# Seven half-size products in place of eight for half of K in two output tile pairs of a two-layer encoder kernel

## What is computed

```python
def _spatial_gating_mixer(h, w_in, ln_g, ln_b, w_s, b_s, w_out):
    ...
    y = u * sv * jax.nn.silu(z)      # (512, 2048)
    return y @ w_out                 # w_out: (2048, 1024)
...
    x = x + gate * y                 # y is here the mixer's result
return _rmsnorm(x, final_g)
```

## Time and profile before

| | us |
|---|---|
| median of 3 runs (803.05 to 803.89) | 803.4 |
| the profiled execution: its time | 802.44 |
| the profiled execution: its span, first to last instruction | 800.6 |
| PE busy | 792.4 |
| DVE busy | 659.4 |
| ACT busy | 455.7 |

### The profile page before, as it was taken

How to read it: one execution, slowest core, us unless ns; L and a number is a source line. 1 busy time by engine, 2 the same in 40 slices (tenths; PEclk the granted TensorE clock), 3 DMA queues, 4 the chain that set the end, 5 groups by cost and what they waited for, 6 DMA issues and landing times.

```text
span 800.6 us, 15179 instructions
## 1 busy us (share of the span) xinstructions
PE 792.4 (99%) x5562; PEld 744.7 (93%) x5562; DVE 659.4 (82%) x954; ACT 455.7 (57%) x638; POOL 82.8 (10%) x108
## 2 busy tenths in 40 slices
PE   9999999999999999999999999999999999999996
PEld 8889999999999999998889888899999999988896
DVE  5989999999999999898896788978888888883334
ACT  4675656565656656572332886656767777762220
POOL 1010000000000000102201241010000000000000
PEclk9999999999999999999999999999999999999999
DMA  9996566666666666589873784255455445454103
GB/s 348 374 204 196 145 184 183 183 183 184 182 185 179 187 177 190 174 247 364 316 246 86 251 239 86 76 142 155 135 154 157 131 131 151 138 194 173 54 1 106
DMA packets 42097, 143.92 MB, mean 180 GB/s; under 512 B 5336, under 2 KB 7638, under 8 KB 42064
## 3 DMA queue, kind: packets, MB, share of 16 engines
q1 hardware_dynamic: 31760, 111.16, 38.4%
q0 software_dynamic: 9152, 30.16, 20.4%
q10 hardware_dynamic: 1152, 2.18, 0.7%
HBM read 109.14 MB, written 4.21 MB: 142 GB/s over the span
## 4 chain that ended last, share of the span: by engine, by line
PE 95%; issue 3%; DVE 1%; ACT 1%; POOL 0%; POOLq 0%; DVEq 0%
PE pp L1363 11%; PE pp L1364 11%; PE pp L1365 11%; PE pp L1222 8%; PE pp L1224 7%; PE pp L1223 7%; PE p_aux L1363 7%; PE p_aux L1364 7%; PE p_aux L1365 7%; PE pp L1318 3%; PE pp L1495 2%; PE pp L1497 2%; PE pp L1496 2%; PE p_aux L1537 2%; PE p_aux L1610 2%
## 5 line engine op out<-in xcount | busy, mean ns | idle before, releaser
L1363 PE MATMUL pp<-h_hi,wh 128*128 128x256 f32 x280 | 79.3, 283 | 0.0
L1364 PE MATMUL pp<-h_lo,wh 128*128 128x256 f32 x280 | 79.2, 283 | 0.0
L1365 PE MATMUL pp<-h_hi,wl 128*128 128x256 f32 x280 | 79.2, 283 | 0.0
L825 ACT ACTIVATE wh<-wt 128x1024 fp32r<-128x1024 f32 x56 | 58.9, 1054 | 13.7 <-DVE wt L1900 7.6
L1919 DVE TENSOR_TENSOR wl<-wt,wh 128x1024 fp32r<-128x1024 f32 x56 | 66.5, 1219 | 0.2 <-ACT wh L825 0.2
L1363 PE MATMUL pp<-s_hi,wh 128*128 128x256 f32 x224 | 63.4, 283 | 0.0
L1364 PE MATMUL pp<-s_lo,wh 128*128 128x256 f32 x224 | 63.4, 283 | 0.0
L1365 PE MATMUL pp<-s_hi,wl 128*128 128x256 f32 x224 | 63.4, 283 | 0.0
L1365 PE MATMUL p_aux<-s_hi,wl 128*128 128x256 f32 x224 | 63.4, 283 | 0.0
L1363 PE MATMUL p_aux<-s_hi,wh 128*128 128x256 f32 x224 | 63.4, 283 | 0.0
L1364 PE MATMUL p_aux<-s_lo,wh 128*128 128x256 f32 x224 | 63.4, 283 | 0.0
(11 more groups left out here) (291 smaller groups left out, 2656.3 us busy)
## 6 DMA issues: line engine op xcount, KB each, us to landing
raw<-in_stream SPq DMA_DIRECT2D x140, 512.0 KB, 4.1
wl<-raw POOLq DMA_DIRECT2D x28, 512.0 KB, 4.5
raw_l<-in_stream SPq DMA_DIRECT2D x18, 512.0 KB, 6.5
raw_s<-in_stream SPq DMA_DIRECT2D x16, 512.0 KB, 13.8
wl_b<-raw POOLq DMA_DIRECT2D x16, 512.0 KB, 4.6
raw_m<-in_stream SPq DMA_DIRECT2D x14, 512.0 KB, 3.3
xv_lo<-y POOLq DMA_DIRECT2D x6, 512.0 KB, 6.0
x_s<-in_xt SPq DMA_DIRECT2D x4, 512.0 KB, 5.9
```

The costliest lines, as they stand in the source:

```text
L825: act.activation(wh[g % 2][:, at], wt[g % 2][:, at], ACT.Copy).then_inc(t_hi_cut, 1)
L1363: pe.matmul(out, hi, hi_of(k), start=fresh and k == 0, stop=False, skip_group_check=not fresh)
L1364: pe.matmul(out, hi, lo_of(k), start=False, stop=False, skip_group_check=not fresh)
L1365: mm = pe.matmul(out, lo, hi_of(k), start=False, stop=k == 3, skip_group_check=not fresh)
```

## The change

For pairs 1 and 2, the upper half of K (K tiles 8 to 15, slots 2 and 3 of the pair) is no longer done as 48 matmuls of 512 columns. It is seen as a 2 x 2 block product: y's upper half in four parts, positions 0-255 and 256-511 by K tiles 8-11 and 12-15 (`y_part(t, kh)`), and the weights in four parts by output tile and K half. Seven products of 12 matmuls with 256 columns (`seventh`) take the place of the eight block products. Slots 0 and 1 stay as they were.

What this needs beside it:

- Once, four sums of parts of y (`s_sum_o_at`, 128x1024 each) on DVE, their high parts on ACT (`hi_s_o`) and low parts on DVE (`s_low_o`). The sums read `y32`; the low parts of K tiles 8 to 11 go to new places, while `y_low` 6 and 7 still overwrite K tiles 12 to 15 and now stand behind three of the sums.
- For each of the two pairs, four sums of weights (`t_sums_o`, one instruction of 128x1024 and two of 128x512), two high parts and two low parts of 128x1024; three copies out of PSUM on ACT (`copy_o`); on DVE the x update in five pieces instead of two.
- The partial results go to banks of `p_aux` besides the pair's own two.

The diff, cut to its core:

```diff
+        so_hi = at_kb("so_hi", 60, [P, 4, 4, HALF], F32R)
+        so_lo = at_kb("so_lo", 76, [P, 4, 4, HALF], F32R)
+        so_f = at_kb("so_f", 76, [P, 4, 4, HALF])
+        to_hi = at_kb("to_hi", 16, [P, 2048], F32R)
+        to_lo = at_kb("to_lo", 188, [P, 2048], F32R)
+        to_f = at_kb("to_f", 188, [P, 2048])
+        y_lo_4 = at_kb("y_lo_4", 24, [P, 2, S], F32R)
+        y_lo_5 = at_kb("y_lo_5", 172, [P, 2, S], F32R)
...
+        bank_a_o, bank_c_o = {1: p_aux[:, 0, :], 2: p_aux[:, 2, :]}, {1: p_aux[:, 1, :], 2: p_aux[:, 3, :]}
...
+            if layer and kt // 2 in (4, 5):
+                return (y_lo_4, y_lo_5)[kt // 2 - 4][:, kt % 2, :]
+            return y_lo[:, kt, :]
...
-            for j in range(DPAIRS - 1):
-                for s in range(4):
-                    cut_hi_late(j + W_BOUT // 4, s, 1)
-                square_x(1, j)
-            cut_hi_late(W_BOUT // 4 + DPAIRS - 1, 0, 1)
...
+            at_w = W_BOUT // 4
+            cut_hi_late(at_w, 0, 1)
+            for n in (0, 1, 3):
+                hi_s_o(n)
+            cut_hi_late(at_w, 1, 1)
+            hi_s_o(2)
+            hi_t_o(1, 0)
+            hi_t_o(1, 1)
+            cut_hi_late(at_w, 2, 1)
+            square_x(1, 0)
+            cut_hi_late(at_w, 3, 1)
+            cut_hi_late(at_w + 1, 0, 1)
+            cut_hi_late(at_w + 1, 1, 1)
+            copy_o(1, 0)
+            cut_hi_late(at_w + 1, 2, 1)
+            copy_o(1, 1)
+            copy_o(1, 2)
+            hi_t_o(2, 0)
+            hi_t_o(2, 1)
...
-            for j in range(DPAIRS - 1):
-                if j == 1:
-                    pe.wait_ge(c_sum_b, OFF + 3 * 2 * PAIRS)
-                out_product(1, W_BOUT, j)
...
+            def seventh(out, stationary, moving, fresh):
+                hi_of, lo_of = moving
+                for k in range(4):
+                    hi, lo = stationary(k)
+                    pe.matmul(out, hi, hi_of(k), start=fresh and k == 0, stop=False, skip_group_check=not fresh)
+                    pe.matmul(out, hi, lo_of(k), start=False, stop=False, skip_group_check=not fresh)
+                    mm = pe.matmul(out, lo, hi_of(k), start=False, stop=k == 3, skip_group_check=not fresh)
+                return mm
...
+            def seven_products(j):
+                a, b, c = bank_a_o[j][:, left], pp[out_bank(1, j)], bank_c_o[j][:, left]
+                for s in range(2):
+                    out_slot(1, W_BOUT, j, s)
+                    for u in range(2):
+                        if s == 0 and j != 1:
+                            pe.wait_ge(x_updated, X_STEPS + FREE + j + u)
+                        unit(pp[out_bank(1, j) + u][:, :], weights(s, u, out_ring[1]), rows(y_hi), low_rows(1),
+                             range(4 * s, 4 * s + 4), s == 0, s == 1).then_inc(blocks, 1)
+                out_slot(1, W_BOUT, j, 2)
+                seventh(a, tile_hi_lo(2, 0), y_own(0, 0), True).then_inc(prod_o, 1)
+                pe.wait_ge(s_cut_o, 1)
+                pe.wait_ge(t_cut_o, of_o(j, 2, 1))
+                seventh(c, t_hi_lo(0), y_summed(N1), True).then_inc(prod_o, 1)
+                pe.wait_ge(s_cut_o, 2)
+                pe.wait_ge(t_cut_o, of_o(j, 2, 2))
+                pe.wait_ge(copied_o, of_o(j, 3, 1))
+                seventh(a, t_hi_lo(2), y_summed(S2), False).then_inc(prod_o, 1)
+                out_slot(1, W_BOUT, j, 3)
+                seventh(b[:, left], tile_hi_lo(3, 0), y_own(0, 1), False).then_inc(prod_o, 1)
+                pe.wait_ge(s_cut_o, 4)
+                pe.wait_ge(copied_o, of_o(j, 3, 2))
+                seventh(a, t_hi_lo(1), y_summed(S3), False).then_inc(prod_o, 1)
+                seventh(b[:, right], t_hi_lo(3), y_own(1, 1), False).then_inc(prod_o, 1)
+                pe.wait_ge(c_22_o, of_o(j, 1, 1))
+                seventh(c, tile_hi_lo(3, 1), y_summed(S4), False).then_inc(blocks, 4)
+            out_product(1, W_BOUT, 0)
+            pe.wait_ge(c_sum_b, OFF + 3 * 2 * PAIRS)
+            pe.wait_ge(sv_used, 2 + KE)
+            for j in B_SEVEN:
+                seven_products(j)
...
+                out = y_lo[:, 2 * n:2 * n + 2, :]
+                if nth >= PAIRS and n in (4, 5):
+                    out = (y_lo_4, y_lo_5)[n - 4][:, :, :]
+                dve.tensor_tensor(out, y32[:, 2 * n:2 * n + 2, :],
...
-            for j in range(DPAIRS - 1):
-                for s in range(4):
-                    if j == 0 and s == 0:
-                        y_low(PAIRS + 6)
-                        y_low(PAIRS + 7)
-                    cut_lo_late(j + W_BOUT // 4, s, 1)
-                if j == 0:
-                    add_gates()
...
+            def s_sum_o_at(n):
+                out = so_f[:, n, :, :]
+                if n == 0:
+                    dve.wait_ge(y_made_b, PAIRS)
+                    ins = dve.tensor_tensor(out, y_part(1, 1), y_part(1, 0), ALU.subtract)
+                elif n == 2:
+                    ins = dve.tensor_tensor(out, y_part(0, 0), y_part(1, 0), ALU.subtract)
+                else:
+                    dve.wait_ge(s_sum_o, (n + 1) // 2)
+                    ins = dve.scalar_tensor_tensor(out=out, in0=so_f[:, n // 2, :, :], scalar=-1.0,
+                                                   in1=y_part(0, n // 2), op0=ALU.mult, op1=ALU.subtract)
+                ins.then_inc(s_sum_o, 1)
...
+            def seven_copied(j):
+                dve.wait_ge(copied_o, of_o(j, 3, 3))
+                n = step(add_to_x(2 * j, pc_b[:, j % 2, 0:2, :].rearrange("p a e -> p (a e)"), gate(1, 2 * j)))
+                dve.wait_ge(prod_o, made_o(j, "Q5"))
+                dve.tensor_tensor(tmp[:, 0, halves[1]], bank_c_o[j][:, 0:HALF], pc_b[:, j % 2, 1, :],
+                                  ALU.add).then_inc(c_22_o, 1)
+                return n
...
+            at_w = W_BOUT // 4
+            cut_lo_late(at_w, 0, 1)
+            for n in (0, 1, 3):
+                s_sum_o_at(n)
+            dve.wait_ge(s_sum_o, 3)
+            y_low(PAIRS + 6)
+            y_low(PAIRS + 7)
+            s_sum_o_at(2)
+            cut_lo_late(at_w, 1, 1)
+            t_sums_o(1)
+            cut_lo_late(at_w, 2, 1)
+            add_gates()
+            after(step(dve.tensor_scalar(gate_neg[:, :], mod[:, 5 * KD:6 * KD], -1.0, None, ALU.mult)))
+            dve.wait_ge(x_back[0], 16)
+            update_x(1, 0, False)
+            s_low_o(1, 0)
+            s_low_o(2, 1)
+            cut_lo_late(at_w, 3, 1)
+            t_low_o(1, 0)
+            t_low_o(1, 1)
+            cut_lo_late(at_w + 1, 0, 1)
+            s_low_o(3, 3)
+            s_low_o(4, 2)
+            square_adds(0)
+            cut_lo_late(at_w + 1, 1, 1)
+            n_1 = seven_plain(1)
+            cut_lo_late(at_w + 1, 2, 1)
+            n_0 = seven_copied(1)
+            seven_first(1, n_0)
+            t_sums_o(2)
+            seven_second(1, n_1)
...
```

More of the change, by code:

```diff
@@ L106 @@
 N_W = 3584
+B_SEVEN = (1, 2)
+SEVEN = {name: n + 1 for n, name in enumerate("Q1 Q5 Q6 Q2 Q7 Q4".split())}
 V_OPS = ("B11", "B21", "T1", "T2", "T3", "T4", "B22")
@@ L381, in of_b, with y_lo_at, made_o, of_o @@
             return 2 * each * i + (each * g + more)
+        def y_lo_at(layer, kt):
+            if layer and kt // 2 in (4, 5):
+                return (y_lo_4, y_lo_5)[kt // 2 - 4][:, kt % 2, :]
+            return y_lo[:, kt, :]
+        def made_o(j, name):
+            return len(SEVEN) * B_SEVEN.index(j) + SEVEN[name]
+        def of_o(j, each, more):
+            return each * B_SEVEN.index(j) + more
+        def landed_o(j):
+            return 16 * (W_BOUT // 4 + j + 15 + UZ_SLOTS // 4)
+        def seven_done(j):
+            return 8 * j + FREE + 2 * W_BOUT + 8
         def landed_b(i):
@@ L1196, in _, with hi_s_o, hi_t_o, copy_o @@
                 y_high_b(n, "Q3")
-            for j in range(DPAIRS - 1):
-                for s in range(4):
-                    cut_hi_late(j + W_BOUT // 4, s, 1)
-                square_x(1, j)
-            cut_hi_late(W_BOUT // 4 + DPAIRS - 1, 0, 1)
+            def hi_s_o(n):
+                act.wait_ge(s_sum_o, (1, 2, 4, 3)[n])
+                act.activation(so_hi[:, n, :, :], so_f[:, n, :, :], ACT.Copy).then_inc(s_hi_cut_o, 1)
+            def hi_t_o(j, n):
+                act.wait_ge(t_sum_o, of_o(j, 3, (1, 3)[n]))
+                at = slice(1024 * n, 1024 * (n + 1))
+                act.activation(to_hi[:, at], to_f[:, at], ACT.Copy).then_inc(t_hi_cut_o, 1)
+            def copy_o(j, n):
+                act.wait_ge(prod_o, made_o(j, ("Q1", "Q6", "Q7")[n]))
+                act.activation(pc_b[:, j % 2, (0, 2, 1)[n], :], bank_a_o[j][:, 0:HALF], ACT.Copy).then_inc(copied_o, 1)
+            at_w = W_BOUT // 4
[17 more added lines that the diff above has]
+            hi_t_o(2, 1)
+            cut_hi_late(at_w + 1, 3, 1)
+            cut_hi_late(at_w + 2, 0, 1)
+            square_x(1, 1)
+            cut_hi_late(at_w + 2, 1, 1)
+            cut_hi_late(at_w + 2, 2, 1)
+            for n in range(3):
```

(71 more changed lines are left out.)

21 lines of the change are left out of this document (17 added, 4 removed).

## The result

| | us |
|---|---|
| before, median of 22 executions beside the changed kernel's | 803.78 (802.72 to 806.38) |
| changed, median of 22 executions | 805.28 (803.91 to 807.68) |
| ratio, 95% interval | 1.0023 (1.0015 to 1.0031) |
| predicted | 804.6 (802.4 to 806.0) |
| span of the profiled execution, before and changed | 800.6 and 803.1 |

What follows compares the result with a forecast made beforehand. The prediction took PE's rate as the bound. Matmul gain -1.62, slot 3 wait +2.05 and `c_22` waits +0.82 gave +1.25 us, added to 803.4 for 804.6 us, range 802.4 to 806.0.

Steps and rivals of the forecast that it cites:

- The bound: In pairs 1 and 2 PE is busy for all of 21.76 us, so its rate sets the span.
- The gain of the matmuls: Pairs 1 and 2: 84 matmuls of 256 columns replace 48 of 512, saving 0.81 us a pair, 1.62 in all.
- The wait at slot 3: Pair 0: PE waits for `y_low` 6 and 7, now behind three sums on DVE; costs 2.05 us.
- The wait at `c_22`: End of pairs 1 and 2: Q3 waits for DVE's `c_22`, behind an x update; 0.41 us a pair, 0.82 in all.
- What was to be hidden: Added DVE work, 23 us against 28 us of room in pairs 1 and 2, and ACT's 10.8 us cost 0.
- The rival of a late DVE: Pair 1: DVE, with only 0.9 us to spare, reaches `c_22` late, costing 0.7 to 1.6 us; chance 0.12.
- The rival of the clock: Pair 0: PE's 2 us standstill lowers the clock for slot 3, adding 5.4 us, to 810; chance 0.05.
- The sum: Whole kernel: -1.62 + 2.05 + 0.82 = +1.25 us, added to the median of 803.4 for 804.6.

Runs made afterwards that it cites:

- Both: Changed kernel with two sums of y moved ahead of slot W+3's low part and `c_22` ahead of the x update on DVE; ratio 0.9978 against before.
- half-width kernel: Kernel before, with the 48 matmuls of 512 columns of slots 2 and 3 in each of pairs 1 and 2 done as 96 of 256; ratio 1.001.

## Why the prediction was right, point by point

- **The bound.** PE's rate: right. In the kernel with both edits PE is busy for all of 63.72 us, and the gain appears in full at the end.
- **The gain of the matmuls.** 1.62 forecast, 1.59 measured (`Both`). The 13 ns beside the columns at either width are confirmed by the half-width kernel, 0.63 and 0.66 us a pair for 48 matmuls more. The gap of the Trainium skill's page ("TensorE: Matmul & The Clock Gate", "Back-to-back issue gap"), by which the gain would have been 2.4, does not hold for these matmuls at the upper level of the clock: 0.2267 and 0.1199 us were measured. At the lower level the distance was 0.43 us for 512 columns, which is the columns alone; there the page agrees.
- **The wait at slot 3.** 2.05 forecast, 2.18 measured (pair 0 is 23.97 against 21.79). PE restarted 2.08 us late, of which the profile shows 1.92 as idle since it draws a matmul longer than the distance to the next, and the second matmul came 0.10 late, as forecast. The difference from the forecast is mostly that PE restarted 0.14 us after `y_low` ended and not 0.05. Found by following DVE one instruction at a time from ACT's high part; removed by two sums moved ahead.
- **The wait at `c_22`.** 0.41 a pair forecast; removing it gave 0.41 a pair. In pair 1 `c_22` ended at 746.41 and Q3 began at 746.47, 1.87 us after Q7's last matmul had started, as forecast; the profile draws 0.16 of the delay of 0.31 as idle.
- **What was to be hidden** was hidden: no wait before Q5, Q6, Q7 or any slot in pairs 1 to 3. DVE's slack before the copies in pair 1 was computed as 0.9 and is 0.96. At the start of pair 2 PE also has to wait for `x_updated`, before and now, which the list of its waits left out; no idle time comes of it.
- **The rival of a late DVE** did not happen, by just that slack.
- **The rival of the clock** is the step that was wrong. The text took the 4 us at the end of the trace of before as the stillness that a fall needs, and so gave 0.05 to a fall after 2 us, with a price of 5.4 us. That was one value from one trace: at the ends of the thirteen traces the clock falls 1.7 to 4.7 us after the last matmul. Within the stage the runs show the fall 4.3 us after the last matmul ended, 2.8 us after it, and 0.8 us behind a wait of 1.93 us; its price is 1.4 to 1.6 us, because the clock was back 3.0 to 4.2 us after PE had restarted and the slot did not run at the lower level to its end. The rule in the Trainium skill (same page, "HAM oscillation — how this bites in real kernels") named the right mechanism; reading a safe length out of a single row was the mistake. That it did not move the median out of the forecast's range is luck: the fall is seen in one profile of five, and it is cheap.
- **The sum.** The pairs give +1.41 where +1.25 was forecast, and the two medians differ by 1.50. Of the 0.7 us between the forecast of 804.6 and the measured 805.28, 0.4 is the starting point: the kernel before measured 803.78 in the 22 executions, where the prediction started from 803.4. The ratio's +1.9 (1.2 to 2.5) has room for the pairs alone and also for a fall in up to a third of the executions (+2.0); which of them it is, the runs do not show.

## What to carry to other kernels

Where one engine sets the pace, list for each operand that it waits for what now stands ahead of it in its maker's queue, and put first what the pacing engine waits for: here 2 us and twice 0.4 us turned a gain of 1.6 us into a loss, and two small reorderings on an engine that is not the bound gave it back. Price a Strassen step with the cost per matmul in the trace and not with columns: halving the width took 0.63 of the 1.44 us that seven for eight gave. And expect a wait of TensorE of about 2 us to cost more than its length in some executions: 1.6 us more in one of the five profiled here.

## What the runs showed of the hardware

- The clock can fall after a wait of only 1.93 us, and after PE has started again (0.8 us later); in 6 of the 7 profiled executions with the same wait it did not. With waits of 2.94 and 8.10 us it fell in the one profile of each; with 2.94 us at least five of the eight timed executions had no fall.
- After a program's last matmul the clock fell 1.7 to 4.7 us later, in thirteen profiles with nearly the same work.
- The price of a fall was 1.4 to 1.6 us after waits of 1.93, 2.94 and 8.10 us.
- At 1.2 GHz matmuls of 512 columns start 0.43 us apart (512 / 1.2 GHz = 0.427), with none of the 13 ns that stand beside the columns at 2.4 GHz (0.2267 against 0.213).
- The restart behind a wait costs about 0.1 us more than the wait: the second matmul starts 0.31 us after the first with 512 columns (0.227 otherwise) and 0.23 with 256 (0.12 otherwise).
